# The readout turns and the tables beside the first MLP stand at later steps of TensorE and ScalarE

## The reference, cut to what matters

```python
for i in range(2):                                  # second block
    h = rmsnorm(x, norm_mix[i])
    mix = diff_attention(h, ...) if i == 0 else s5_mixer(h, ...)
    x = x + mix
    x = x + sqrelu_mlp(rmsnorm(x, norm_mlp[i]), mlp_w1[i], mlp_w2[i])
...
def sqrelu_mlp(h, w1, w2):                          # 2048 -> 8192 -> 2048
    a = jax.nn.relu(h @ w1)
    return (a * a) @ w2

def s5_mixer(h, a_re, a_im, log_dt, b_re, b_im, c_re, c_im, d_skip, w_glu):
    ...                                             # 128 groups of 16 channels and 64 states
    bu = u @ bb                                     # complex; bb from b, a and dt
    x = scan(x -> a x + bu)                         # over 256 tokens, complex
    y = Re(x @ c) + d_skip * h
    val, gate = split(gelu(y) @ w_glu)
    return val * sigmoid(gate)
```

## Time and profile before

| | |
|---|---|
| runs | 3109.2, 3109.37, 3111.38 us (median 3109.37) |
| the profiled execution | 3105.89 us, its span 3104.1 us |
| TensorE busy | 2931.8 us, 94% |
| VectorE busy | 1873.7 us, 60% |
| ScalarE busy | 1454.9 us, 47% |
| GpSimd busy | 367.0 us, 12% |
| mean granted TensorE clock | 0.979 |
| weights and data moved | 550 MB, 177 GB/s in the mean |

### The profile page before, as it was taken

One profiled execution on the slowest core, in us unless ns is written; L12 is line 12 of the kernel. 1 busy time (PEld: TensorE's weight loads), 2 busy tenths in 40 slices (PEclk: granted clock), 3 DMA queues, 4 the chain that ended last, 5 costly groups with the idle time before them and its releaser, 6 DMA issues.

```text
span 3104.1 us, 45330 instructions
## 1 busy us (share of the span) xinstructions
PE 2931.8 (94%) x19056; PEld 2666.1 (86%) x19056; DVE 1873.7 (60%) x2604; ACT 1454.9 (47%) x1996; POOL 367.0 (12%) x444
## 2 busy tenths in 40 slices
PE   8999899998999999994988999989899999999998
PEld 8989888987889988984978999878788999999996
DVE  5996655754565555872455565567555555555555
ACT  5335545444455455441344464447644544444443
POOL 0000000000000000088476300014000000000000
PEclk9999999999999999997999999999999999999999
DMA  6555355432555545574556655544455555555553
GB/s 229 174 189 177 123 194 172 163 107 74 199 176 168 175 163 176 179 242 163 188 198 205 208 184 197 190 151 153 146 193 176 195 192 190 192 190 190 189 189 125
DMA packets 266570, 550.05 MB, mean 177 GB/s; under 512 B 9152, under 2 KB 13376, under 8 KB 266112
## 3 DMA queue, kind: packets, MB, share of 16 engines
q1 hardware_dynamic: 260192, 522.88, 50.5%
q0 software_dynamic: 5456, 21.73, 1.8%
q10 hardware_dynamic: 720, 2.55, 0.2%
HBM read 526.15 MB, written 20.97 MB: 176 GB/s over the span
## 4 chain that ended last, share of the span: by engine, by line
PE 70%; DVE 12%; POOL 7%; DMA 5%; ACT 4%; issue 2%; ACTq 0%; SPq 0%; DVEq 0%; POOLq 0%
PE G L476 66%; DVE WL L1511 4%; POOL TS L2243 4%; PE T L476 3%; DVE Y L1519 3%; DMA RD<-s_r 2%; POOL TC L2243 2%; DMA s_r<-TC 1%; DMA s_w<-TS 1%; ACT WH L977 1%; ACT US L974 1%; PE T L526 1%; DVE TC L1511 0%; DVE US L2121 0%; DVE ST L1586 0%
## 5 line engine op out<-in xcount | busy, mean ns | idle before, releaser
L1511 DVE TENSOR_TENSOR WL<-RAW,WH 128x1024 fp32r<-128x1024 f32 (+1 forms) x948 | 1172.3, 1245 | 907.1 <-ACT WH L977 896.1
L977 ACT ACTIVATE WH<-RAW 128x1024 fp32r<-128x1024 f32 (+1 forms) x948 | 992.0, 1055 | 1115.7 <-PE G L476 1106.7
L476 PE MATMUL G<-A1h,WH 128*128 128x256 f32 x2560 | 726.4, 284 | 22.9 <-DVE WL L1511 22.6
L476 PE MATMUL G<-A1l,WH 128*128 128x256 f32 x2560 | 718.8, 281 | 0.0
L476 PE MATMUL G<-A1h,WL 128*128 128x256 f32 x2560 | 718.6, 281 | 0.0
L476 PEld LDWEIGHTS G<-A1h,WH 128*128 128x128 f32 x2560 | 489.1, 191 | 26.2 <-issue 15.7
L476 PEld LDWEIGHTS G<-A1h,WL 128*128 128x128 f32 x2560 | 489.6, 191 | 0.0
L476 PEld LDWEIGHTS G<-A1l,WH 128*128 128x128 f32 x2560 | 487.5, 190 | 0.8
L476 PE MATMUL G<-WH,Bh 128*128 128x512 f32 x1024 | 400.3, 391 | 9.6 <-DVE WL L1511 9.6
L476 PE MATMUL G<-WL,Bh 128*128 128x512 f32 x1024 | 399.4, 390 | 0.0
L476 PE MATMUL G<-WH,Bl 128*128 128x512 f32 x1024 | 399.3, 390 | 0.0
(11 more groups left out here) (314 smaller groups left out, 3628.5 us busy)
## 6 DMA issues: line engine op xcount, KB each, us to landing
RAW<-in_mlp_w SPq DMA_DIRECT2D x256, 1024.0 KB, 5.4
RAW<-in_even_w_in SPq DMA_DIRECT2D x56, 1024.0 KB, 5.1
RAW<-in_a_w_in SPq DMA_DIRECT2D x48, 1024.0 KB, 5.1
RAW<-in_b_w_glu SPq DMA_DIRECT2D x32, 1024.0 KB, 5.3
RAW<-in_odd_w_in SPq DMA_DIRECT2D x20, 1024.0 KB, 5.0
RAW<-in_even_w_out SPq DMA_DIRECT2D x16, 1024.0 KB, 5.1
RAW<-in_odd_w_out SPq DMA_DIRECT2D x16, 1024.0 KB, 5.1
RAW<-in_a_w_out SPq DMA_DIRECT2D x16, 1024.0 KB, 5.1
```

What stands on the lines that cost most here:

```text
L476: return e.matmul(out, lhsT, rhs, start=start, stop=stop, skip_group_check=True)
L977: return e.activation(out, in_, ACT.Copy, scale=scale, bias=0.0)
L1511: return e.tensor_tensor(out, a, b, op)
```

## The change

The steps of the four readout turns go from 60, 76, 92, 108 to 92, 115, 138, 161, and so ScalarE's copies, eight items behind, go from 68, 84, 100, 116 to 100, 123, 146, 169. The four table calls go from 160, 164, 168, 172 to 200, 201, 202, 203; with the six items that each call adds they start at items 160, 170, 180, 190 before and 200, 207, 214, 221 after. The programs of VectorE, GpSimd and SP are the same, and so are all instructions of TensorE and ScalarE but for their place.

```diff
@@ -449,8 +449,8 @@
     TOP_O = [(s, i) for i in range(2) for s in (0, 2, 4, 6, "marks")] + [("mask", 0), ("mask", 1)]
-    C_STEPS = (60, 76, 92, 108)
-    T_STEPS = (160, 164, 168, 172)
+    C_STEPS = (92, 115, 138, 161)
+    T_STEPS = (200, 201, 202, 203)
```

## The result

| | before | after |
|---|---|---|
| median of the runs (us) | 3109.28 (4 runs) | 3033.27 (3029.78 to 3035.44, 4 runs) |
| span of the profiled execution | 3104.1 | 3030.7 |
| mean granted clock | 0.979 | 0.988 |

The ratio is 0.9755, with a 95% interval of 0.9738 to 0.9772: 76 us less. 3033.4 had been forecast. The two profiled executions shown here and ahead of the prediction differ by 73.4 us in their spans.

A forecast was written before the change was run, and what follows sets the result against it. GpSimd was taken to stop TensorE in the first MLP: 44.4 + 24.0 us of waits and 7.5 of slow clock, 76 us in all. 3109.4 - 76 = 3033.4 us; range 3029 to 3043, a little over 8 in 10.

The forecast's parts named there:

- What bounds it: First MLP, halves 60 to 239: TensorE waits on GpSimd, 44.4 + 24.0 us idle, plus 7.5 us of slow clock.
- The number: Forecast median of the changed kernel: 3109.4 - 76 = 3033.4 us.
- The pace: Halves 60 to 239 undisturbed: 2.77 us a half plus 0.9 for each of four transpose sets, 499 us.
- First turning: Step 92: GpSimd's mask ready at 1499.3, 20 us ahead of TensorE at 1519, so the 44.4 us wait goes.
- The cycle: Between ScalarE's copies: GpSimd's mask and four readout steps take 60.2 us against 62.5 of spacing, so 24.0 us go.
- The tables: ScalarE's table steps from 200: argument product ready at 1802, step reached at 1820, 18 us to spare, no cost.
- FD: GpSimd's clearing of FD waits for half 239: 132 us before, about 45 us after.
- the groups outlast the spacing: Rival at ScalarE's copies: GpSimd's groups take 65 to 75 us, giving back 5 to 30 us, 3038 to 3063; chance 0.09.
- The lock at its extreme: Rival: each GpSimd product waits out a whole VectorE WL, taking 1.9 us; slower, 3134 us; chance 0.01.

The follow-up runs named there:

- experiments 2 and 3: Against the changed kernel: 2, turns at 92, 108, 124, 140 (old spacing), 3067.43 us; 3, turns at 60, 83, 106, 129 (old first turn), 3077.22 us.
- experiment 4: Changed kernel with the four table calls at steps 170, 174, 178, 182 instead of 200 to 203: 3071.92 us.
- Experiment 7: Changed kernel, halves 28 to 88: VectorE makes only 8 of 1024 WL columns, 3039.37 us; or copies RAW to WL instead, 3032.03 us; one run each.
- the copy: Changed kernel in which VectorE copies RAW to WL, one SBUF input instead of two, for halves 28 to 88: 3032.03 us in one run.
- experiment 5: Changed kernel with the turns at 84, 107, 130, 153, the first eight halves earlier at the same spacing: 3043.22 us.
- experiment 8: Changed kernel with VectorE's parameter steps over three halves instead of two, turns at 102, 125, 148, 171, tables at 205 to 208: 3028.11 us, again 3026.76.

## Why the prediction was right, point by point

- *What bounds it.* Four waits, 68.4 us idle and 7.5 of clock. Each part put back alone brought its own share, 31.0 and 47.4 us against 30 and 46 expected from the same terms. The sums fit better than their terms: the waits came out 7 us larger together and the clock 3.5 us smaller (experiments 2 and 3). In the kernel before, TensorE's busy time was 6.9 us above that after, which is the 7.5.
- *The number.* That the median fell 0.1 us from the forecast is luck. The spans of the two profiled executions differ by 73.4 us, not 76, and the kernel before had medians from 3102.3 to 3110.2 us in the later groups. What the working could promise was its range.
- *The pace.* 179 halves of 2.77 us and four sets of transposes made 499 us; 500.4 were measured, and 499.3 to 500.4 in four executions of two kernels without a wait.
- *First turning.* The mask was forecast ready at 1499.3 with TensorE at 1519: 1501.9 and 1520.4. Two sizes were off against each other, the steps (11.2 us, not 10.7) and the mask (1.9 us, not 3.9). By other executions the date lay up to 13 us earlier or 4 later.
- *The cycle.* 60.2 us were set against 62.5. The groups took 54.6 to 59.2 and left 5 to 10 us. The caution of taking the last group of before for all was right in direction and some us too large.
- *The tables.* Argument ready forecast 1802, step at 1820: 1799.4 and 1822.5. *FD* 45 us: 46.4.
- *One statement was wrong*, though no term rested on it. I wrote that at the old place, step 160, ScalarE would wait 90 us. By the program it would wait for ever (no run had it): the product it needs follows GpSimd's last group, which waits for ScalarE's copies of step 169, behind it on the same queue. Table steps may only stand behind the last copies, and right behind them they still cost 36 us of TensorE (experiment 4). The two tuples are one schedule.
- *The rivals.* That the groups outlast the spacing could be brought about only by setting it to 20, and then cost 1.9 us; at 16 it cost 31. The lock at its extreme did not come: the product beside VectorE takes 1.15 us, not 1.9. Experiment 7 shows VectorE's work to be what slows GpSimd's products, as read, but only about 1.7 of the 4.6 us by which a drive step was faster in the pause. The prediction put all of that on VectorE's quiet; most of the rest was the transfers, fast while no weights were loaded. No term of the sum rested on it, since the steps were taken at their pace beside the running MLP, which holds both. The rule of the Trainium skill (SBUF — State Buffer, "SBUF: two separate sides") names VectorE instructions with two SBUF inputs, and those in a two-port mode, as the ones that collide with GpSimd. The trace agrees for the first kind (1151 against 653 ns), though such means don't show whether the loser waits out the whole instruction; the copy slowed GpSimd as well (777), but no run here shows in which mode it ran.

## What to carry to other kernels

When side work is written into an engine's queue by hand, every item has a date at which its data is ready and a date at which the queue gets there; read both off the trace in units of the main loop, and put the item where the first is ahead of the second by more than the spread between executions. A handshake that comes back (copy, group, copy) is a cycle with a period of its own, and its spacing must hold the whole period, not only its first item. Take the producer's pace from where the other engines and the weight loads run beside it, and never from a pause that the change will remove.

## What had not been expected of the hardware

- GpSimd's date for the same instructions moves by 18 us between executions: the last drive step is issued at 1486.2 us in one trace of the changed kernel and at 1499.3 in another, and at 1503.7 in that of experiment 5, whose program is the same up to there. Both its instructions and its waits for landings differ: in the two traces of the changed kernel the 64 products of the drive steps took 69.3 and 64.3 us, and the waits for s_w 17.6 and 10.1. That the phase of GpSimd against VectorE's WL and the weight loads decides it was not tested.
- The S5 stage behind the MLP sets a part of the spread of the runs. With the same instructions, the part behind half 239 took 1098.7 us in the changed kernel's profiled execution and 1108.4 in that of experiment 5; between two executions of one and the same kernel, that of experiment 8, it was 1099.0 and 1103.8. The clock tells them apart: the same 45 us, first of the changed kernel, then of experiment 5.

```profile
1976.00:2021.00 45.00, 36.50 (x274) 33.73 (x273) 27.76 (x64) 19.74 (x44) 12.36 (x19) 0.92 0.32 112
```

```profile
1985.00:2030.00 45.00, 37.19 (x213) 33.53 (x211) 22.05 (x55) 16.08 (x36) 9.10 (x14) 0.73 0.24 84
```

  There TensorE works in short pieces between waits of the S5 chain and drops to 1.2 GHz for more or less of it; in the second it did 213 products in the time of 274. So one profiled execution can stand 5 us above another of the same kernel, and perhaps the whole 10, for a reason that no edit made, and the stretch of the edit must be compared by itself, as was done here.
